# VectorE's first low part of a kept tile, moved in front of the choice step and the W_q half

## The reference

```python
def _peer(h, w_q, subkeys, u, v):
    q = (ht @ w_q).reshape(t, PEER_HEADS, 2, PEER_HALF)
    sc = jnp.einsum("thcd,hckd->thck", q, subkeys).astype(jnp.float32)
    s1, i1 = lax.top_k(sc[:, :, 0], PEER_TOPK)
    s2, i2 = lax.top_k(sc[:, :, 1], PEER_TOPK)
    cand = (s1[..., :, None] + s2[..., None, :]).reshape(t, PEER_HEADS, PEER_TOPK * PEER_TOPK)
    top, idx = lax.top_k(cand, PEER_TOPK)
    ...
    act = jax.nn.gelu(jnp.einsum("tkd,td->tk", ug, hb), approximate=False) * gb.astype(hb.dtype)
    return jnp.einsum("tk,tkd->td", act, vg)
```

## Time and profile before

| what | us |
|---|---|
| median of three runs | 3031.75 (3031.33 to 3032.7) |
| the profiled execution | 3034.17 |
| its span | 3032.4 |
| TensorE busy | 2932.0 |
| VectorE busy | 2338.6 |
| ScalarE busy | 1011.9 |
| GpSimd busy | 1506.8 |

### The profile page before, as it was taken

One profiled execution on the slowest core, in us unless ns is written; L12 is line 12 of the kernel. 1 busy time (PEld: TensorE's weight loads), 2 busy tenths in 40 slices (PEclk: granted clock), 3 DMA queues, 4 the chain that ended last, 5 costly groups with the idle time before them and its releaser, 6 DMA issues.

```text
span 3032.4 us, 40835 instructions
## 1 busy us (share of the span) xinstructions
PE 2932.0 (97%) x15249; PEld 2610.0 (86%) x15249; DVE 2338.6 (77%) x3102; ACT 1011.9 (33%) x1245; POOL 1506.8 (50%) x906
## 2 busy tenths in 40 slices
PE   8999999999999999999999999999999999999998
PEld 6888777788889999999999999999997778877777
DVE  5444767754588888888888897898767989988998
ACT  3222333331323323333333332333223333333333
POOL 1000223200026656565565655466857878886752
PEclk9999999999999999999999999999999999999999
DMA  7877677777459998989899898899999999999998
GB/s 262 265 237 220 217 251 232 231 271 254 129 188 309 322 322 295 341 297 315 303 321 327 295 349 276 304 326 334 322 352 387 414 414 413 415 415 415 416 415 326
DMA packets 321775, 947.11 MB, mean 312 GB/s; under 512 B 62484, under 2 KB 179232, under 8 KB 232288
## 3 DMA queue, kind: packets, MB, share of 16 engines
q1 hardware_dynamic: 177040, 475.04, 43.5%
q0 software_dynamic: 107008, 439.75, 40.8%
q10 hardware_dynamic: 37584, 30.43, 3.1%
HBM read 849.56 MB, written 95.55 MB: 312 GB/s over the span
## 4 chain that ended last, share of the span: by engine, by line
PE 69%; DVE 13%; DMA 12%; issue 3%; ACT 3%; ACTq 0%; DVEq 0%; SPq 0%; POOL 0%
PE ps L1724 21%; PE ps L1726 21%; PE ps L1725 21%; DMA v_raw<-in_peer_v 9%; PE ps L1974 4%; DVE x_rows L1586 2%; DMA wc_raw<-in_w_in 2%; DVE v_lo L1629 2%; DVE u_row L1575 2%; ACT v_hi L1109 1%; DVE uT_lo L1569 1%; DMA gates_of<-gate_grid 1%; DVE uT_lo L1564 1%; PE ps L1824 1%; DVE seg_turned L1226 1%
## 5 line engine op out<-in xcount | busy, mean ns | idle before, releaser
L1724 PE MATMUL ps<-hT_hi,uT_hi 128*128 128x384 f32 x2048 | 703.6, 344 | 20.1 <-DVE uT_lo L1564 18.1
L1726 PE MATMUL ps<-h2T_lo,uT_hi 128*128 128x384 f32 x2048 | 689.1, 336 | 0.0
L1725 PE MATMUL ps<-hT_hi,uT_lo 128*128 128x384 f32 x2048 | 687.7, 336 | 0.0
L759 POOL DMA_INDIRECT gate_grid<-gates,grid_cells x256 | 538.1, 2102 | 107.4 <-issue 78.8
L1724 PE MATMUL ps<-v_hi,a_hi 128*128 128x512 f32 x1024 | 406.5, 397 | 40.6 <-DVE v_lo L1629 36.7
L1724 PEld LDWEIGHTS ps<-hT_hi,uT_hi 128*128 128x128 f32 x2048 | 386.8, 189 | 28.4 <-DVE uT_lo L1564 21.9
L1725 PE MATMUL ps<-v_hi,a_lo 128*128 128x512 f32 x1024 | 404.1, 395 | 0.0
L1726 PE MATMUL ps<-v_lo,a_hi 128*128 128x512 f32 x1024 | 403.8, 394 | 0.0
L1109 ACT ACTIVATE v_hi<-v_raw 128x2048 fp32r<-128x2048 f32 x128 | 245.6, 1919 | 461.0 <-PE ps L1726 316.0
L1725 PEld LDWEIGHTS ps<-hT_hi,uT_lo 128*128 128x128 f32 x2048 | 387.1, 189 | 1.9
L1726 PEld LDWEIGHTS ps<-h2T_lo,uT_hi 128*128 128x128 f32 x2048 | 386.3, 189 | 0.0
(11 more groups left out here) (206 smaller groups left out, 4968.2 us busy)
## 6 DMA issues: line engine op xcount, KB each, us to landing
v_raw<-in_peer_v SPq DMA_DIRECT2D x128, 1024.0 KB
u_tile<-in_peer_u SPq DMA_DIRECT2D x88, 1024.0 KB
seg_rows<-in_peer_u SPq DMA_DIRECT2D x40, 1024.0 KB, 6.4
u_tile<-uT_all SPq DMA_DIRECT2D x40, 1024.0 KB
uT_all<-seg_turned SPq DMA_DIRECT2D x100, 256.0 KB, 6.5
w_raw<-in_w_in SPq DMA_DIRECT2D x24, 1024.0 KB, 6.6
wc_raw<-in_w_in SPq DMA_DIRECT2D x48, 512.0 KB, 7.4
gate_grid<-zeros POOLq DMA_DIRECT2D x16, 1024.0 KB
```

Source lines behind the costliest of these rows:

```text
L759: pool.indirect_dma_start(out=gate_grid, out_offset=bass.IndirectOffsetOnAxis(ap=grid_cells[:, d, col:col + 1], axis=0), in_=gates[:, 2 + ...
L1724: mm(out, a_hi, b_hi, start=first, stop=False)
L1725: mm(out, a_lo, b_hi, start=False, stop=False)
L1726: return mm(out, a_hi, b_lo, start=False, stop=last)
```

## The change

In a step c > 0 whose next tile, c + 1, is kept turned (c = 2, 4, ..., 78; b is even), VectorE makes the low part of that tile's first half at the head of the step, in front of the choice and of the W_q half. Before, it stood behind both. The other steps, and all other engines' orders, stay as they are.

```diff
                 for b in range(TOPK):
                     c = TOPK * i + b
+                    kept = c > 0 and turned_before(c + 1)
+                    if kept:
+                        split_u(c + 1, 0)
                     if choosing:
                         choose(i + 1, b, 0)
                     if querying and b - 1 in SPLIT_WQ:
                         split_wq(i + 2, SPLIT_WQ.index(b - 1), half=0)
                     if last and b == TOPK - 1:
                         weigh_pair(0)
-                    elif c > 0:
+                    elif c > 0 and not kept:
                         split_u(c + 1, 0)
                     if c > 0:
                         dot(c - 1)
```

## The result

The changed kernel takes 3042.14 us (median of 6 runs, 3041.39 to 3046.42) against 3031.54 us for the kernel before beside it (6 runs, 3028.75 to 3032.99): a ratio of 1.0037 [1.0025, 1.0049], 10.6 us slower. The forecast was 13.5 us slower, 3045.2 us. The profiled execution took 3042.34 us, its span 3040.5.

A forecast was written before the change was run, and what follows sets the result against it. TensorE bounds the kernel, waiting in places for VectorE, which has fallen behind as a whole. The terms, -4.4 + 7.9 + 10 = +13.5 us on the 3031.75 us median, gave 3045.2 us, range 3034 to 3053.

The forecast's parts named there:

- the one at b = 0: TensorE's stall at b = 0: 0.87 us gained at tile 17, swallowed before the second half of tile 19.
- b = 8: Tiles 9, 25, 41, 57, 73: VectorE idles for ScalarE's high part, second half late; 5 x 1.58 = 7.9 us lost.
- The moved stall at b = 2: At b = 2 TensorE's wait moves from before the first half to before the second, for 2.9 to 3.7 us.
- one sign of being wrong: Wrong if tile 19's second half ends earlier, against tile 14's second half, than 1084.38 against 1030.21.
- The clock: Behind the five long stalls at b = 2 the clock falls, 2.0 us each: 10 us lost, between 8 and 14.
- The gain of 4.4 us: Returned by moving the stall at b = 2, by head: 1.0 + 1.0 + 1.0 + 1.4 + 0.
- (a): Rival: the waits move as forecast but the clock doesn't fall for them; +3.5, 3035.2 us; chance 0.12.
- (b): Rival: the stall at b = 8 drops the clock too, adding up to 8 us; 3053 us; chance 0.15.
- (c): Rival: ScalarE's high part is ready at b = 8, so no idle time; without falls 3027.4 us; chance 0.08.
- (d): Rival: nothing changes, as the moved product lies on no path; 3031.8 us; chance 0.05.
- The skill's rule: Rule cited against the clock term: by it the moved stall at b = 2 costs no clock; 3.5 us lost in all.
- The other steps: Steps at b = 4, 6, 10, 12 and 14 cost nothing; without cover, 15 to 20 late by up to 1.5 us each.

The follow-up runs named there:

- b = 8 kernel: The kernel before with the first half's low part moved to the head of the step at b = 8 only; 3033.79 us, ratio 1.0021.
- "others" kernel: The kernel before with the move at b = 4, 6, 10, 12 and 14 only; 3029.36 us, ratio 1.0000.
- filled kernel: The changed kernel with 18 unread matmuls added ahead of TensorE's wait for the second half at b = 3; 3029.57 us, ratio 1.0004.

## Why the prediction was right, point by point

**Direction and mechanism: right.** The stall at b = 2 moved from the first to the second half, the one at b = 0 went and was swallowed, b = 8 got a new one, and every other step was free: the four parts timed alone give +6.4 (b = 8), +4.2 (b = 2), -0.3 (b = 0) and 0.0 us (others), 10.3 together, where the whole gives 10.6 (each with some 3 us of uncertainty).

**b = 8: right in kind, too high by 1.1 us.** Forecast 5 x 1.58 = 7.9, found 6.8. VectorE's idle time was right (1.56 us). The failed step is "from being free to the second half's start were 7.72 us without a gap", carried over as it stood. Of the 7.72 some 0.15 was the choice's first operation waiting behind the row update. With the low part between them this wait falls away: from 1146.10 to 1153.67 are 7.57 us. That makes the step 1.4 us. The last head's was 1.12 because there the trace of before is the odd one: TensorE had already waited 0.23 us for the second half of tile 73, and was 5.51 us from half to half instead of the 5.20 of the other heads. The changed kernel has 6.63 there, as at tile 57.

**The moved stall at b = 2: right.** I had "for 2.9 to 3.7 us"; the trace has 3.40 at tile 19, and 3.39 to 3.73 over the five heads. The rows of VectorE ended near where I said (1084.19 against the forecast 1084.38). By its letter one sign of being wrong came true, in small: counted from the start of tile 14's second half it is 53.92 us against 54.17. The step itself kept its sum, 9.07 against 9.05; the 0.25 us were gained ahead of it, mostly at c = 16, where the hoisted product fills a wait of 0.18 us that VectorE had there. So the statement that moving the product changes "the order among them" and not "their sum" holds to some 0.2 us, not exactly. Head 0, the one stall without a fall, shows the gain that I gave each head: -0.99 against -1.0.

**The clock: right in sum, wrong in both factors.** I took "all five" falls at 2.0 us each, 10 us. Found were four. From the second half's first matmul to the transposes took 910.46 - 906.18 = 4.28 us at tile 3, without a fall, and 1090.10 - 1084.24 = 5.86 at tile 19; at tiles 35, 51 and 67 it took 6.84, 6.99 (1451.80 - 1444.81) and 6.89. That is 1.6, 2.6, 2.7 and 2.6 us, 9.5 in all and 2.4 each. The failed step is "Behind all nine idle times above 2.1 us that the trace has, the clock fell, so I count all five". Nine cases without an exception didn't make a certainty of it, as tile 3 shows. The table at the end has more such cases. The price missed by choosing the value "nearer to the row of this stage", a fall behind 2.07 us of idle time, though the row behind 3.65 us was nearer in the length of the idle time; three of the four falls were of its kind, 6.8 us. The two errors cancel.

**The gain of 4.4 us: not visible apart, but borne out.** It stood mostly for falls that the kernel before had and that go with its stalls, and these vary between executions (four in the profile shown; the old stalls of the b = 8 kernel gave two, of the "others" kernel one). In the table b = 0 and 2 give +4.9 where the terms gave -4.4 + 10 = +5.6. With the falls prevented, the filled kernel's +2.63 fits -4.4 + 6.8.

**The rivals.** (a), no falls, is what the filled kernel became; in the changed one four falls decide against it. (b), the b = 8 stalls drop the clock too: none of the five did. (c) had the high part ready at b = 8: VectorE waits 1.56 us for it. (d) is out by the interval.

**The skill's rule.** The Trainium skill (page "TensorE: Matmul & The Clock Gate", section "Loop structure matters more than you think") says that VectorE's copying of results doesn't break the array's warmth, and says it of a loop whose next matmuls follow immediately. I had stretched that to a TensorE that stands waiting for VectorE, and got 3.5 us lost. The rows are against the stretched rule: the clock fell at four of five such waits, and at none in the same place with 18 matmuls in the wait.

**The other steps: right.** The kernel with them alone shows it. One row I misread: of VectorE's idle times before the halves of tile 21, the 1.38 us is marked as ended by issue, not by ScalarE; nothing in the sum hangs on it.

**The last stage** was to be "as long as before" and was 2.7 us shorter in the profiled execution, so the span grew by only 8.1 us. The medians differ by 10.6, and the stage up to tile 80 by 11.25.

## What to carry to other kernels

When an engine's queue holds two products for one consumer, look at which of them is asked for last, and add up what stands in front of that one: moving the first product ahead within the same sum moves the stall and doesn't shorten it. What helps is to put work that nobody waits for, here two W_q halves of 1.22 us, behind the last product asked for; then the same hoist that lost 10.6 us is part of a kernel that gains 17.6. Without the hoist that kernel gained 10.0, and how much of the difference is the hoist's stays open between the shifts and the timed runs. A product put at the head of a queue must also have its input by then, and two short stalls can be cheaper than one long one, since the long one can cost clock on top.

## What the runs showed of the hardware

I had expected the fall of the clock to follow from the length of the idle time alone. Over a wide range it doesn't. These are TensorE's idle times between 865 and 1800 us in all twelve traces, and whether the granted clock was 0.50 behind them:

| idle time ahead, us | falls | of | length of the fall |
|---|---|---|---|
| 1.1 to 1.7 | 0 | 56 | - |
| 1.8 to 1.9 | 1 | 3 | 3.4 us |
| 1.9 to 2.3 | 4 | 11 | 3.4 us |
| 2.5 to 3.2 | 11 | 12 | 3.4 us, one 6.8 |
| 3.3 to 3.8 | 9 | 11 | 3.4 us three times, 6.8 six times |

The falls come in two lengths, of 3.4 and 6.8 us. The short one costs a second half 1.3 to 1.6 us, the long one 2.6 to 2.8 us. It isn't twice as much, since each of the seven long ones begins while TensorE still waits: at tile 51 at 1443.93, 0.9 us before the second half starts. With 18 matmuls (3.37 us) in idle times of 3.4 us the clock stayed at 1.00 in all five. Why the same idle time of 3.39 us at the same tile is followed by a fall in one kernel and by none in the other, is left open here. For a single trace it means an uncertainty of several us: a fall that comes or doesn't moves what follows by some 1 to 3 us.
